# A hybrid decoder layer's HGRN2 head in blocks of 128 tokens, its steps one granule sooner, and the down stage ended bank by bank

## The chip, the cores and the metric

One Trainium2 chip; the program runs on one core of it. The metric is the device time of an execution in microseconds. The profile is that of one execution, which has a time of its own.

## The reference

One inference step of one decoder layer, for a prompt of 256 tokens and for 8 samples of 8 tokens each with a cache of 2048 positions: T = 320 tokens in all, D_MODEL = 2048. What is computed, cut to what matters:

```python
h = rms_norm(x, norm_mix_pre); u = h @ w_in          # columns: hq hf hi hgate dq dk dv g_hg g_da
# HGRN2, per head (8 heads, dk = dv = 128), chunks of c = 64 tokens
f = lb + (1 - lb) * sigmoid(hf); kin = 1 - f; G = cumsum(log f) within a chunk
qg = q * exp(G); kg = kin * exp(-G)
A = where(causal, qg @ kg.T, 0); o = A @ v + qg @ S_prev
dS = (kin * exp(G_last - G)).T @ v; S = exp(G_last) * S_prev + dS       # chunk after chunk
# differential attention: softmax(map 0) - lam * softmax(map 1), times v; over the cache for the samples
y = (sigmoid(g_hg) * (o_hg @ w_branch_hg) + sigmoid(g_da) * (o_da @ w_branch_da)) @ w_out
x = x + rms_norm(y, norm_mix_post)
gate, up = split(rms_norm(x, norm_ffn_pre) @ w_ffn_up)                   # D_FF = 5632
x = x + rms_norm((silu(gate) * up) @ w_ffn_down, norm_ffn_post)          # y_prompt, y_sample
# also out: new keys and values, and the recurrent states (hgrn_prompt, hgrn_sample)
```

## The kernel before, in words

Everything is held transposed: channels on the 128 partitions, the 320 tokens along the free dimension (256 of the prompt, then 64 of the samples). Weights stream in as granules of 128 x 1024 numbers. ACT copies a granule into w_hi (rounded to a shorter float), DVE forms w_lo = raw - w_hi, and TensorE adds the three products hi*hi, lo*hi and hi*lo: 24 matmuls of 320 columns for each granule. There are 4 pairs of buffers (HALVES), so ACT may split granule r once TensorE has used granule r - 4; the semaphores are hi_ready, lo_ready and granule_used. Each engine has its order of work written out by hand, in Python loops that are unrolled and in Fori loops on the chip.

After seven sets of eight granules come eight rounds, one for each head and sample (act_round, vec_round, pe_round, lines 853 to 975). A full round has granules A0 to A7 (a merge-gate set), then D0 to D7 (the next head's set); the last round has no D. Between granules TensorE does the small work of head r (pe_head(q) stands behind granule Aq) and the attention of sample r over its 16 cache pages: scores(g) behind A1, A3, A5 and D0, turn() with 16 transposes of the probabilities behind D2, values(g) behind D3 to D6. On ACT and DVE, act_head(q) and vec_head(q) stand behind the split of granule Aq; vec_head(9) behind D1's split and vec_head(10) behind D2's. vec_pages "most" (lines 759 to 764) forms the row maximum once the last scores are copied, ACT's L708 is the exponential, and turn() waits for it.

The small work of a head, in the names of the code: "i_t" and "kd_t" turn values and decayed keys to have tokens on partitions, five transposes of 64 tokens each; "a" are five products kg x qg; copy_predicated puts them under a causal mask into aT; "ds" are four products that give each chunk's state sum; state[1..4] follow on DVE; "pv" is the attention of the prompt; "ds_s0" and "ds_s1" (lines 624 and 628) give the state sums of samples 0 to 3 and 4 to 7; "o" (lines 632 to 638) sums masked products, states and, for the samples, s0. new_state (line 540) forms the samples' new states, four DVE operations for each half.

At the end, the down stage goes over 44 granules twice (down, line 1213), with eight banks for eight output tiles in each pass. act_out copies the banks into ffn, act_out_sq squares them, vec_squares sums, a product with ones sums over partitions (line 1440), root and reciprocal follow, and four parts of four tiles are scaled, added to the residual and stored (lines 1397 to 1404, 1275).

## Time and profile before

| what | us |
|---|---|
| median of 3 runs | 2168.47 (2166.37 to 2170.33) |
| profiled execution | 2171.54 |
| its span, first to last instruction | 2170.0 |
| TensorE busy (PE) | 2089.6 (96%) |
| weight loads (PEld) | 1954.7 (90%) |
| VectorE busy (DVE) | 1048.1 (48%) |
| ScalarE busy (ACT) | 809.2 (37%) |
| GpSimd busy (POOL) | 74.1 (3%) |

A busy share is the time in which at least one instruction of the engine ran, over the span. Matmuls are pipelined: one of 320 columns is shown 309 ns long but the next begins 147 ns after it, so busy time says that the engine had work, not how fast it went; the distance from start to start does. The granted clock (PEclk) is TensorE's, as a share of 2.4 GHz. PE is the matmuls, PEld the weight loads. Rows of the timeline merge instructions of one line that follow each other on one engine. The seven full rounds lie between 216 and 865 us, the last to 943; branches and output projection follow to 1190, the up projection from there, and the down stage ends at 2140.

### The profile page before, as it was taken

The page shows a single profiled execution, that of the slowest core. Times are in us where ns is not written, and L with a number is a line of the kernel's source. Part 1 is how long each engine was busy: PE and PEld are TensorE (multiplying, and loading weights), DVE is VectorE, ACT ScalarE, POOL GpSimd, SP SyncE. Part 2 cuts the span into 40 slices and gives each one's busy share as a digit, 9 for nine tenths or more (in the row PEclk, how much of TensorE's full clock was granted, in tenths as well). Part 3 has the DMA queues.
Part 4 walks back from the last instruction along what each step waited for, and adds up shares of the span by engine and source line. Part 5 has one row for each costly group of instructions (what it writes and reads, how often), then busy time and mean ns, then how long its engine had stood idle before and what let it go on. Part 6 is the DMA issues. An engine that isn't in the chain of part 4 may idle for free.

```text
span 2170.0 us, 38477 instructions
## 1 busy us (share of the span) xinstructions
PE 2089.6 (96%) x14722; PEld 1954.7 (90%) x14722; DVE 1048.1 (48%) x1323; ACT 809.2 (37%) x1051; POOL 74.1 (3%) x118
## 2 busy tenths in 40 slices
PE   7999999999999999969998899999999999999994
PEld 6999878888888888759998899999999999999994
DVE  6433544536455354555544644444444445445445
ACT  5323343424335242344333433233333333445432
POOL 1001010010100101000000000000000000000000
PEclk9999999999999999989999999999999999999997
DMA  7777686968769687765643244444444444444431
GB/s 251 163 235 240 253 326 246 358 253 338 292 255 354 257 338 298 270 249 193 230 150 124 91 155 146 153 155 155 145 150 149 146 154 144 147 154 145 150 121 48
DMA packets 123842, 443.85 MB, mean 205 GB/s; under 512 B 14485, under 2 KB 18597, under 8 KB 123728
## 3 DMA queue, kind: packets, MB, share of 16 engines
q1 hardware_dynamic: 113872, 403.78, 52.2%
q0 software_dynamic: 9920, 39.38, 6.1%
q8 instruction: 33, 0.54, 0.1%
q14 instruction: 17, 0.14, 0.0%
HBM read 423.19 MB, written 22.54 MB: 205 GB/s over the span
## 4 chain that ended last, share of the span: by engine, by line
PE 92%; DVE 3%; DMA 2%; ACT 1%; issue 1%; DVEq 0%; SPq 0%; ACTq 0%
PE ps L388 23%; PE ps L390 22%; PE ps L389 22%; PE ps L1432 5%; PE ps L1431 5%; PE ps L1433 5%; PE ps L809 3%; DMA raw<-w_in 2%; PE ps L843 2%; PE ps L638 1%; PE ps L818 1%; DVE n_rs L776 0%; PE ps L632 0%; DVE w_lo L347 0%; PE ps L634 0%
## 5 line engine op out<-in xcount | busy, mean ns | idle before, releaser
L347 DVE TENSOR_TENSOR w_lo<-raw,w_hi 128x1024 fp32r<-128x1024 f32 x416 | 504.5, 1223 | 587.3 <-ACT w_hi L342 293.6
L388 PE MATMUL ps<-x_hi,w_hi 128*128 128x320 f32 x1408 | 454.3, 323 | 17.7 <-DVE w_lo L347 10.6
L388 PE MATMUL ps<-h_hi,w_hi 128*128 128x320 f32 x1408 | 436.0, 310 | 11.2 <-DVE h_lo L1371 10.6
L389 PE MATMUL ps<-x_hi,w_lo 128*128 128x320 f32 x1408 | 442.0, 314 | 0.0
L390 PE MATMUL ps<-x_lo,w_hi 128*128 128x320 f32 x1408 | 441.5, 314 | 0.0
L389 PE MATMUL ps<-h_hi,w_lo 128*128 128x320 f32 x1408 | 435.1, 309 | 0.0
L390 PE MATMUL ps<-h_lo,w_hi 128*128 128x320 f32 x1408 | 435.0, 309 | 0.0
L342 ACT ACTIVATE w_hi<-raw 128x1024 fp32r<-128x1024 f32 x240 | 250.3, 1056 | 417.6 <-PE ps L390 417.6
L388 PEld LDWEIGHTS ps<-x_hi,w_hi 128*128 128x128 f32 x1408 | 271.4, 193 | 64.3 <-issue 49.2
L388 PEld LDWEIGHTS ps<-h_hi,w_hi 128*128 128x128 f32 x1408 | 264.6, 188 | 13.2 <-ACT stage L1307 11.5
L389 PEld LDWEIGHTS ps<-x_hi,w_lo 128*128 128x128 f32 x1408 | 271.6, 193 | 0.0
L390 PEld LDWEIGHTS ps<-x_lo,w_hi 128*128 128x128 f32 x1408 | 270.9, 192 | 0.0
L389 PEld LDWEIGHTS ps<-h_hi,w_lo 128*128 128x128 f32 x1408 | 264.7, 188 | 0.2
L390 PEld LDWEIGHTS ps<-h_lo,w_hi 128*128 128x128 f32 x1408 | 264.6, 188 | 0.0
L1431 PE MATMUL ps<-hid_hi,w_hi 128*128 128x320 f32 x704 | 217.3, 309 | 0.0
L1432 PE MATMUL ps<-hid_hi,w_lo 128*128 128x320 f32 x704 | 217.2, 309 | 0.0
L1433 PE MATMUL ps<-hid_lo,w_hi 128*128 128x320 f32 x704 | 217.2, 309 | 0.0
L370 ACT ACTIVATE w_hi<-raw 128x1024 fp32r<-128x1024 f32 x120 | 126.1, 1051 | 114.6 <-DMA raw<-w_in 98.1
L1431 PEld LDWEIGHTS ps<-hid_hi,w_hi 128*128 128x128 f32 x704 | 132.0, 187 | 0.1
L1433 PEld LDWEIGHTS ps<-hid_lo,w_hi 128*128 128x128 f32 x704 | 132.0, 187 | 0.0
L1432 PEld LDWEIGHTS ps<-hid_hi,w_lo 128*128 128x128 f32 x704 | 132.0, 187 | 0.0
L1383 DVE TENSOR_TENSOR hid_lo<-hidden,hid_hi 128x320 fp32r<-128x320 f32 x88 | 43.3, 492 | 154.8 <-ACT w_hi L1322 154.4
(261 smaller groups left out, 2314.2 us busy)
## 6 DMA issues: line engine op xcount, KB each, us to landing
raw<-w_in SPq DMA_DIRECT2D x176, 512.0 KB, 7.4
raw<-w_up SPq DMA_DIRECT2D x176, 512.0 KB, 3.3
raw<-ck SPq DMA_DIRECT2D x128, 512.0 KB, 6.1
raw<-cv SPq DMA_DIRECT2D x128, 512.0 KB, 7.1
raw<-w_dn SPq DMA_DIRECT2D x88, 512.0 KB, 3.3
raw<-w_out SPq DMA_DIRECT2D x32, 512.0 KB, 4.2
uT<-stage POOLq DMA_DIRECT2D x14, 640.0 KB, 3.7
raw<-w_hg SPq DMA_DIRECT2D x16, 512.0 KB, 4.4
```

The lines of the kernel that those rows point to most:

```text
L342: act.activation(w_hi[slot % HALVES][:, :], raw[slot][:, :], ACT.Copy).then_inc(hi_ready, 1)
L347: dve.tensor_tensor(w_lo[half][:, :], raw[slot][:, :], w_hi[half][:, :].bitcast(F32), ALU.subtract).then_inc(lo_ready, 1)
L370: act.activation(w_hi[q % HALVES][:, :], raw[ring_of(r).slot[kind, q]][:, :], ACT.Copy).then_inc(hi_ready, 1)
L388: pe.matmul(out, wh[:, c, m, :], xh(c), start=first, stop=False)
L389: pe.matmul(out, wl[:, c, m, :], xh(c), start=False, stop=False)
L390: mm = pe.matmul(out, wh[:, c, m, :], xl(c), start=False, stop=last)
L809: ins = pe.matmul(ps[32 * j:32 * j + 32, 7, :], q_rows[:, h, :], raw_all[:, at:at + QUAD, h * PAGE:(h + 1) * PAGE], start=e == 0, stop=e == 1)
L843: ins = pe.matmul(ps[32 * j:32 * j + 32, 6, 0:2 * DV], p_keys[:, p, 32 * j:32 * j + 32], raw[slot][:, 2 * DV * j:2 * DV * (j + 1)], start= ...
L1383: dve.tensor_tensor(hid_lo[slot % HALVES][:, :], hidden[:, bass.ds(k, 1), :].rearrange("p a t -> p (a t)"), hid_hi[slot % HALVES][:, :].bi ...
L1431: pe.matmul(ps[:, m, 0:T], wh[:, c], xh, **dict(add, start=q == 0))
L1432: pe.matmul(ps[:, m, 0:T], wl[:, c], xh, **add)
L1433: ins = pe.matmul(ps[:, m, 0:T], wh[:, c], xl, **dict(add, stop=q >= 3))
```

## The change

In the head, the tokens are taken in blocks of 128, 128 and 64 instead of five of 64: i_tok, kd_tok, aT and the mask are [128, ...]. i_t and kd_t are three transposes each, "a" three products under a mask that is zero outside the two chunks on the diagonal. The state sums of two chunks of one block are products over rows 0 to 63 and rows 64 to 127, into banks 4 and 6. The two sums of the samples are products over rows 0 to 31 and 32 to 63, into banks 6 and 5, with one own_part instead of two. The bank of "a" and of pd's transposes is 5, pv's is 6. Each step stands one granule sooner where it can: kd_t and a behind A3, ds and pd_t behind A4, pv behind A5, the chunks' o behind A6, the samples' part and ds_s behind A7. vec_head(9) only copies o; vec_head(10) forms all eight new states.

In the down stage, the last three granules of the second pass are taken together, bank after bank, with nine products for each bank and granule triple; the last turn of the loop is written out for it. ACT squares each bank from PSUM as it is done, DVE adds each square. The sum product is two of 160 columns in banks 0 and 1. ffn's first eight tiles have been scaled by their gains between the passes (act_out_gain), so the first two output parts need one operation of 1280 columns; the other eight are scaled straight from PSUM. The last part of four tiles is two of two.

```diff
@@ act_head
             if q == 4:
                 act.wait_ge(h_pe.sem, h_pe.at(h, "i_t"))
-                act.activation(i_tok[:, 0:4, :], ps[0:CHUNK, 6, :].rearrange("p (c d) -> p c d", c=4), ACT.Copy)
-                h_act.done(act.activation(i_tok[:, 4, :], ps[0:CHUNK, 4, 3 * P:4 * P], ACT.Copy), "i_tok")
+                h_act.done(by_token(act, i_tok, 6), "i_tok")
+            if q == 5:
+                act.wait_ge(h_pe.sem, h_pe.at(h, "kd_t"))
+                h_act.done(by_token(act, kd_tok, 4), "kd_tok")
             if q == 6:
...
+                act.wait_ge(h_pe.sem, h_pe.at(h, "pd_t"))
...
+        def by_token(act, dst, bank):
+
+            act.activation(dst[:, 0:2, :], ps[:, bank, 0:2 * P].rearrange("p (c d) -> p c d", c=2), ACT.Copy)
+            return act.activation(dst[0:CHUNK, 2, :], ps[0:CHUNK, bank, 2 * P:3 * P], ACT.Copy)
@@ vec_head
-            if q == 4:
+            if q == 3:
                 dve.wait_ge(h_act.sem, h_act.at(h, "eG"))
...
             if q == 9:
                 dve.wait_ge(h_pe.sem, h_pe.at(h, "o"))
-                new_state(0, 6)
                 h_vec.done(dve.tensor_copy(o_hg[:, bass.ds(h, 1), :].rearrange("p a t -> p (a t)"),
                                            ps[:, 4, 0:T]), "o")
             if q == 10:
-                dve.wait_ge(h_pe.sem, h_pe.at(h, "ds_s1"))
-                new_state(1, 5)
+                dve.wait_ge(h_pe.sem, h_pe.at(h, "ds_s"))
+                new_state(0, 6)
+                h_vec.done(new_state(1, 5), "s_new")
@@ pe_head
-            if q == 4:
+            if q == 3:
                 pe.wait_ge(h_vec.sem, h_vec.at(h, "qkd"))
...
+                h_pe.done(to_tokens(kd, 4), "kd_t")
+                for t0, n in NT:
+                    ins = pe.matmul(ps[0:n, 5, t0:t0 + n], kg[:, t0:t0 + n], qg[:, t0:t0 + n], start=True, stop=True)
+                h_pe.done(ins, "a")
+            if q == 4:
                 pe.wait_ge(h_act.sem, h_act.at(h, "kd_tok"))
                 for c in seq:
-                    ins = pe.matmul(ps[:, 4, c * DV:(c + 1) * DV], kd_tok[:, c, :], i_tok[:, c, :],
-                                    start=True, stop=True)
+                    at = c // 2 * DV
+                    ins = pe.matmul(ps[:, 4 + 2 * (c % 2), at:at + DV], kd_tok[rows[c], c // 2, :],
+                                    i_tok[rows[c], c // 2, :], start=True, stop=True)
                 h_pe.done(ins, "ds")
...
+                for j, (t0, n) in enumerate(NT):
+                    pe.matmul(ps[:, 4, t0:t0 + n], i_tok[0:n, j, :], aT[0:n, t0:t0 + n], start=True, stop=True)
+                    for c in ((1,), (2, 3), ())[j]:
+                        pe.matmul(ps[:, 4, span[c]], state[:, c - 1, :], qg[:, span[c]], start=False, stop=True,
+                                  skip_group_check=True)
             if q == 7:
...
                 h_pe.done(ins, "o")
+                pe.wait_ge(h_act.sem, h_act.at(h, "o_att"))
+                for b in range(2):
+                    t = slice(32 * b, 32 * b + 32)
+                    ins = pe.matmul(ps[:, 6 - b, :], kd_tok[t, 2, :], i_own[t, :, :], start=True, stop=True)
+                h_pe.done(ins, "ds_s")
@@ down
+                turns = (DOWN - 4) // 8 - pas
+                with eng.Fori(0, turns) as i:
                     for q in range(4, 12):
-                        one(8 * i + q, q, i)
+                        one(8 * i + q, q, i, do)
+                if pas:
+                    for q in range(4, 12):
+                        one(8 * turns + q, q, turns, end if end and q > 11 - MERGED else do)
...
+        def act_out_gain(act):
+            act.wait_ge(g_act.sem, g_act.at(0, "q1"))
+            for m in range(8):
+                ins = act.activation(ffn[:, m, :], ffn[:, m, :], ACT.Copy, scale=nrm_w[:, 3, m:m + 1])
+            g_act.done(ins, "w")
...
+        def act_end_sq(act):
+
+            act.wait_ge(g_vec.sem, g_vec.at(0, "s1"))
+            for m in range(8):
+                if m < 7:
+                    act.wait_ge(down_done, 7 * 5 + 7 * 4 + m + 1)
+                else:
+                    act.wait_ge(granule_used, R_DOWN + 2 * DOWN)
+                t_act.done(act.activation(stage[m // 4][:, m % 4, :], ps[:, m, 0:T], ACT.Square), f"q{m}")
+
+        def vec_end_sq(dve):
+            for m in range(8):
+                dve.wait_ge(t_act.sem, t_act.at(0, f"q{m}"))
+                t_vec.done(dve.tensor_tensor(sq_sum[:, :], sq_sum[:, :], stage[m // 4][:, m % 4, :], ALU.add), f"s{m}")
...
@@ act_rest
                 if pas and q == 1:
-                    act_out(act, 0)
+                    act_out(act)
+                if pas and q == 2:
+                    act_out_sq(act)
                 if pas and q == 3:
-                    act_out_sq(act, 0)
+                    act_out_gain(act)
@@ pe_rest
+            def down_end(pas, k, r, slot, use, q):
+
+                if q < 11:
+                    return
+                pe.wait_ge(lo_ready, r + 1)
+                for m in range(8):
+                    c = slice(P * m, P * m + P)
+                    for back in range(MERGED - 1, -1, -1):
+                        at = (slot - back) % HALVES
...
```

How instructions stand on the engines. The first place is VectorE in a full round, from the split of D1 to the end of the maximum (L760 is "near", L764 the negated maximum; L347, L349 are splits). Before:

```order
L347 TENSOR_TENSOR w_lo<-raw,w_hi 128x1024 [waits hi_ready]
L540 SCALAR_TENSOR_TENSOR s<-s,eG,ps 128x128 [waits h_pe]
L540 SCALAR_TENSOR_TENSOR s<-s,eG,ps 128x128 x3
L565 COPY o_all<-ps 128x320
L347 TENSOR_TENSOR w_lo<-raw,w_hi 128x1024 [waits hi_ready]
L540 SCALAR_TENSOR_TENSOR s<-s,eG,ps 128x128 [waits h_pe]
L540 SCALAR_TENSOR_TENSOR s<-s,eG,ps 128x128 x3
L760 TENSOR_TENSOR s_all<-ps,near 128x128 [waits k_act]
L762 TENSOR_REDUCE mxk<-s_all 128x1 [waits k_vec]
```

And of the change, the same stretch:

```order
L349 TENSOR_TENSOR w_lo<-raw,w_hi 128x1024 [waits hi_ready]
L564 COPY o_all<-ps 128x320
L349 TENSOR_TENSOR w_lo<-raw,w_hi 128x1024 [waits hi_ready]
L540 SCALAR_TENSOR_TENSOR s<-s,eG,ps 128x128 [waits h_pe]
L540 SCALAR_TENSOR_TENSOR s<-s,eG,ps 128x128 x7
L759 TENSOR_TENSOR s_all<-ps,near 128x128 [waits k_act]
L761 TENSOR_REDUCE mxk<-s_all 128x1 [waits k_vec]
```

The four states that stood behind D1's split now stand behind D2's, ahead of the maximum.

The second place is TensorE behind granule A7 of a round: the end of the head's part. Before (its last sample sum, L628, stands behind D0 and the scores L809):

```order
L632 MATMUL ps<-aT,i_tok 128x64 [waits h_vec]
L632 MATMUL ps<-aT,i_tok 128x64
L634 MATMUL ps<-qg,state 128x64
...
L635 MATMUL ps<-aT,i_tok 128x64
L638 MATMUL ps<-qg,s 128x8 x8
...
L809 MATMUL ps<-raw,q_rows 32x512 [waits k_act]
L809 MATMUL ps<-raw,q_rows 32x512 x7
...
L628 MATMUL ps<-i_own,kd_tok 128x512 [waits h_vec]
```

Of the change, from behind A6 to behind A7:

```order
L625 MATMUL ps<-aT,i_tok 128x128
L627 MATMUL ps<-qg,state 128x64
L625 MATMUL ps<-aT,i_tok 128x128
L627 MATMUL ps<-qg,state 128x64 x2
L625 MATMUL ps<-aT,i_tok 128x64
...
L632 MATMUL ps<-qg,s 128x8 x8
...
L638 MATMUL ps<-i_own,kd_tok 128x512 [waits h_act]
L638 MATMUL ps<-i_own,kd_tok 128x512
```

The chunks' part has moved one granule up, and both sample sums stand behind the eight-column products (L632 in the change).

The third place is ScalarE at the end of the program (L1237, L1245 before, L1266 after; L1332 and L1354 are the root). Before:

```order
L1237 ACTIVATE ffn<-ps 128x320 [waits down_done] x7
L1237 ACTIVATE ffn<-ps 128x320 [waits granule_used]
L1245 ACTIVATE stage<-ffn 128x1280 [waits g_vec,g_act]
L1245 ACTIVATE stage<-ffn 128x1280
L1332 ACT_TABLE_LOAD
L1332 ACTIVATE rs_mix<-ps,eps_c 128x320 [waits y_pe]
```

Of the change:

```order
L1266 ACTIVATE stage<-ps 128x320 [waits down_done,g_vec]
L1266 ACTIVATE stage<-ps 128x320 [waits down_done] x6
L1266 ACTIVATE stage<-ps 128x320 [waits granule_used]
L1354 ACT_TABLE_LOAD
L1354 ACTIVATE rs_mix<-ps,eps_c 128x320 [waits y_pe]
```

Copies and squares have become one step for each bank.

## Rows read from the trace of the kernel before

**Rows 1.** Windows: stretch, its us, busy time (instructions) by engine, PEclk, DMA share, GB/s.
```profile
654.53:747.32 92.79, 92.74 (x709) 77.08 (x707) 45.58 (x81) 36.51 (x59) 6.31 (x10) 0.96 0.79 297
747.32:838.72 91.40, 91.16 (x709) 75.47 (x707) 45.58 (x81) 36.57 (x59) 6.34 (x10) 0.98 0.80 304
728.75:735.58 6.83, 6.83 (x30) 6.83 (x30) 1.52 (x5) 0.00 (x0) 0.00 (x0) 0.50 0.20 73
824.32:827.74 3.42, 3.42 (x15) 3.42 (x14) 0.66 (x2) 0.00 (x0) 0.00 (x0) 0.50 0.00 0
925.70:930.10 4.40, 3.68 (x16) 3.27 (x16) 0.65 (x1) 1.30 (x3) 0.00 (x0) 0.50 0.72 259
930.13:933.50 3.37, 2.97 (x53) 1.80 (x57) 0.77 (x3) 1.89 (x3) 0.00 (x0) 1.00 0.31 86
```

**Rows 2.** Timeline, TensorE, rounds 4 and 5: start us, us, engine, line, shapes, count.
```profile
637.28 1.95 PE L638 MATMUL ps<-qg,s 128*128 128x8 f32 x16
...
713.11 1.16 PE L611 MATMUL ps<-i_tok,kd_tok 64*128 64x128 f32 x8
...
725.68 0.66 PE L632 MATMUL ps<-aT,i_tok 64*128 64x64 f32 x4
726.27 0.43 PE L634 MATMUL ps<-qg,state 128*128 128x64 f32 x2
...
728.45 3.34 PE L638 MATMUL ps<-qg,s 128*128 128x8 f32 x16
...
738.97 1.12 PE L628 MATMUL ps<-i_own,kd_tok 64*128 64x512 f32 x2
...
747.16 1.91 PE L818 MATMUL ps<-ident,s_all 128*128 128x128 f32 x16
```

**Rows 3.** Timeline, TensorE, the two maps' scores of the prompt, round 5.
```profile
687.73 0.50 PE L590 MATMUL ps<-mk,mq 64*128 64x128 f32 x4
688.06 0.61 PE L591 MATMUL ps<-mk,mq 64*128 64x256 f32 x4
```

**Rows 4.** Timeline, VectorE and ScalarE ahead of turn(), round 5.
```profile
741.81 1.12 DVE L540 SCALAR_TENSOR_TENSOR s<-s,eG,ps 128x128 f32<-128x128 f32 x4
...
742.84 0.28 DVE L760 TENSOR_TENSOR s_all<-ps,near 128x128 f32<-128x128 f32 x1
...
744.27 2.02 ACT L708 ACTIVATE s_all<-s_all,mxk 128x2056 f32<-128x2056 f32 x1 [3.64 <-DVE mxk L764]
...
747.35 1.23 DVE L347 TENSOR_TENSOR w_lo<-raw,w_hi 128x1024 fp32r<-128x1024 f32 x1 [3.12 <-ACT w_hi L370]
```

**Rows 5.** Timeline, between the two down passes; the last is granule q = 4's first product.
```profile
1988.54 2.43 ACT L1245 ACTIVATE stage<-ffn 128x1280 f32<-128x1280 f32 x2
...
1990.45 2.50 DVE L1104 TENSOR_REDUCE sq_part<-stage 128x320 f32<-128x1280 f32 x1
...
1997.26 1.22 DVE L1385 TENSOR_TENSOR w_lo<-raw,w_hi 128x1024 fp32r<-128x1024 f32 x1
...
1999.47 0.31 PE L1431 MATMUL ps<-hid_hi,w_hi 128*128 128x320 f32 x1
```

**Rows 6.** Timeline, the end of the program.
```profile
2137.39 3.52 ACT L1237 ACTIVATE ffn<-ps 128x320 f32<-128x320 f32 x8 [9.48 <-PE ps L1433]
...
2143.39 1.28 ACT L1332 ACT_TABLE_LOAD   x1
...
2147.50 0.49 DVE L1106 TENSOR_TENSOR sq_sum<-sq_sum,sq_part 128x320 f32<-128x320 f32 x1
2148.05 1.44 PE L1440 MATMUL ps<-sq_sum,ones 128*128 128x320 f32 x2 [7.62 <-DVE sq_sum L1106]
...
2150.15 2.15 DVE L1397 RECIPROCAL rs_mix<-rs_mix 128x320 f32<-128x320 f32 x1 [2.16 <-ACT rs_mix L1332]
2152.34 1.94 DVE L1400 SCALAR_TENSOR_TENSOR ffn<-ffn,nrm_w,rs_mix 128x320 f32<-128x320 f32 x4
...
2164.81 1.49 DVE L1404 TENSOR_TENSOR ffn<-o_all,ffn 128x1280 f32<-128x1280 f32 x1
```

More of the change, by code:

```diff
@@ L282, in build @@
         HEAD_LOADS = 16 * 6
-        h_pe = Steps(sem("h_pe"), "scores vk i_t kd_t a ds pd_t pv ds_s0 o ds_s1", 1)
+        h_pe = Steps(sem("h_pe"), "scores vk i_t kd_t a ds pd_t pv o ds_s", 1)
         h_act = Steps(sem("h_act"), "ef tok lg eG p i_tok kd_tok pdt o_att", 1)
-        h_vec = Steps(sem("h_vec"), "fg kin s max nmax G Gd qkd rc rcl pd2 pd own0 aT st1 st2 st3 st4 own1 s_new0 o s_new1", 1)
+        h_vec = Steps(sem("h_vec"), "fg kin s max nmax G Gd qkd rc rcl pd2 pd own aT st1 st2 st3 st4 o s_new", 1)
         passed = sem("passed")
@@ L574, in pe_head, with to_tokens @@
             span = [slice(CHUNK * c, CHUNK * (c + 1)) for c in range(CHUNKS)]
-            def five(src, bank, rest, col):
+            rows = [slice(CHUNK * (c % 2), CHUNK * (c % 2) + CHUNK) for c in seq]
+            def to_tokens(src, bank):
                 pe.sem_inc(passed, 1)
-                for c in range(CHUNKS):
-                    out = ps[0:CHUNK, bank, c * P:(c + 1) * P] if c < 4 else ps[0:CHUNK, rest, col:col + P]
-                    ins = pe.transpose(out, src[:, span[c]], ident[:, :])
+                for j, (t0, n) in enumerate(NT):
+                    ins = pe.transpose(ps[0:n, bank, j * P:(j + 1) * P], src[:, t0:t0 + n], ident[:, :])
                 return ins
@@ L598, in pe_head @@
                 pe.wait_ge(h_act.sem, h_act.at(h, "tok"))
-                pe.wait_ge(h_vec.sem, h_vec.at(h, "s"))
-                h_pe.done(five(x[:, 2, :], 6, 4, 3 * P), "i_t")
-            if q == 4:
-                pe.wait_ge(h_vec.sem, h_vec.at(h, "qkd"))
-                pe.wait_ge(h_act.sem, h_act.at(h, "i_tok"))
-                h_pe.done(five(kd, 4, 5, T), "kd_t")
-                for c in range(CHUNKS):
-                    ins = pe.matmul(ps[0:CHUNK, 5, span[c]], kg[:, span[c]], qg[:, span[c]], start=True, stop=True)
-                h_pe.done(ins, "a")
@@ L1436, in down_granule @@
                 ins.then_inc(granule_used, 1)
-            down(pe, down_granule)
-            pe.wait_ge(g_vec.sem, g_vec.at(1, "s1"))
-            y_pe.done(pe.matmul(ps[:, 0, 0:T], ones[:, :], sq_sum[:, :], start=True, stop=True), "ss")
+            def down_end(pas, k, r, slot, use, q):
[6 more added lines that the diff above has]
+                        at = (slot - back) % HALVES
+                        xh, xl = hid_hi[at][:, :], hid_lo[at][:, :]
+                        add = dict(start=False, stop=True, skip_group_check=True)
+                        pe.matmul(ps[:, m, 0:T], w_hi[at][:, c], xh, **add)
+                        pe.matmul(ps[:, m, 0:T], w_lo[at][:, c], xh, **add)
+                        ins = pe.matmul(ps[:, m, 0:T], w_hi[at][:, c], xl, **add)
+                        if m == 7:
+                            ins.then_inc(granule_used, 1)
+                    if m < 7:
+                        ins.then_inc(down_done, 1)
+            down(pe, down_granule, down_end)
+            pe.wait_ge(t_vec.sem, t_vec.at(0, "s7"))
+            for e in range(2):
+                own = slice(T // 2 * e, T // 2 * e + T // 2)
+                ins = pe.matmul(ps[:, e, T:T + T // 2], ones[:, :], sq_sum[:, own], start=True, stop=True)
+            y_pe.done(ins, "ss")
         def pool_rest(pool):
@@ L1690 @@
     same = (i[:, None] // NQ == i[None, :] // NQ).astype(np.int32)
+    causal = np.zeros((P, T), np.int32)
+    for c in range(SEQ // CHUNK):
+        t0 = c % 2 * CHUNK
+        causal[t0:t0 + CHUNK, CHUNK * c:CHUNK * c + CHUNK] = tri
+    causal[0:CHUNK, SEQ:T] = tri * same
     hot = np.zeros((33, BIAS_L), np.float32)
```

162 lines of the change are left out of this document (73 added, 89 removed).

## The prediction

> **What bounds the kernel now.** I read the stretches by window first. They show the profiled execution's 93 us rounds: TensorE is busy in all of both rounds shown (92.74 of 92.79 us, 91.16 of 91.40), VectorE in half, and the difference between the two rounds is clock: 0.96 against 0.98 granted [rows 1]. Then the timeline of one round, r = 5. So what TensorE is given to do, at which clock, and the few places where it has no slack decide a round. Seven rounds are full ones; the eighth has no granules D. At the end of the program nothing overlaps any more: from the last product on, the last copies, squares, sums, root, reciprocal and four output parts follow each other [rows 6].
>
> Two facts of these rows carry the argument. First the clock. In round 5 TensorE runs at 0.50 (1.2 of 2.4 GHz) from 728.75 to 735.58, in round 6 from 824.32 to 827.74 [rows 1]. Each fall comes while TensorE is in, or just behind, its sparsest stretch, the state block after granule A7: small products L632 to L635 and then L638 with eight columns each. The 16 instructions of L638 take 1.95 us at full clock and 3.34 us when it fell [rows 2]. Half clock costs half its duration, so 3.4 us in round 5 and 1.7 in round 6. The two rounds differ by 1.39 us, near the 1.7 of the difference. By their lengths and clock the seven full rounds have five long falls and two short ones: 5 x 3.4 + 2 x 1.7 = 20.5 us, 2.9 a round. Second, a chain at turn(): scores s3 end at 738.97 (the start of L628), ACT copies them and splits D2's weights, DVE splits D2, forms four states (L540), corrects and reduces the row maximum (from L760), ACT takes the exponential L708, and only then may TensorE transpose (L818) [rows 2, 4].
>
> **The change part by part, in a full round.**
>
> Products. L611 has 8 instructions in 1.16 us at K = 64, so about 0.11 us each beyond the first latency [rows 2].
> - i_t, kd_t and a: ten transposes become six, five products three. Eight instructions fewer, some of them 64 columns wide: estimate -0.4 us.
> - ds keeps its four products, but neighbours now stand in rows 0 to 63 and 64 to 127, with different banks. The scores do that already: L590 and L591, eight instructions of 128 and 256 columns, span from 687.73 to 688.67, 0.94 us [rows 3], where at the 0.11 us per 128 columns of L611 they would need 0.4 + 0.9 + latency 0.2 = 1.5. Pairs run beside each other. I take -0.45; the bounds are 0 and -0.55 (half of 1.1).
> - o: the pieces before L638 go from 725.68 to 728.45, 2.77 us, for 16 instructions. Two of one kind cost about 0.16 + 0.20, because each change between K = 64 and K = 128 shows up: L632 at 725.68 (four) needs 0.59, L634 0.36 [rows 2]. After: 12 instructions, one such change instead of seven, 12 x 0.11 + 0.25 = 1.56. That is -1.2.
> - Sample states: L624 and L628 are two instructions each, 1.05 us before the next may start (L628 shows 1.12 with its tail) [rows 2], 2.1 together. After, two products of K = 32 in rows 0 to 31 and 32 to 63, banks 6 and 5. Taken as a pair: 1.1 us, -1.0. Bounds 0 and -1.05. For K = 32 no row exists, the nearest is the K = 64 pair of [rows 3].
>
> The Trainium skill, "TensorE: Matmul & The Clock Gate", Part 3, lets small products in different row groups run concurrently, K = 32 included; by it the last line would be exactly one product's time, 1.05. The trace agrees for K = 64 and has nothing for K = 32.
>
> Sum of the products: -0.4 - 0.45 - 1.2 - 1.0 = -3.05 us a round.
>
> The turn. L628 stood behind s3 and took 1.05 us of TensorE there; it is now ahead of D0. TensorE then reaches turn() 747.16 - 738.97 - 1.05 = 7.14 us after s3. The chain does not get shorter, it gets longer: new_state(0) has left its idle place in D1 and stands between D2's split and L760, so eight L540 instead of four. Four take 742.84 - 741.81 = 1.03 us [rows 4]. Queued behind them on DVE are the maximum, for which ACT waits, and D3's split. L708 ended at 744.27 + 2.02 = 746.29, 7.3 us after s3, with the readout of its sum 7.4; now 8.4. TensorE waits 1.3 us. Its transposes (1.7 us to the next start, 1.91 with the tail [rows 2]) end at 10.1; D3's split L347 ended at 747.35 + 1.23 = 748.58 [rows 4], 9.6 after s3, now 10.65. TensorE waits 0.55 more. Together +1.9 us. This is the stall that replaces the work taken away. Bounds: 0 (if the order on DVE turned out harmless) and 2.6. Per round -3.05 + 1.9 = -1.15; seven rounds -8.0.
>
> Steps one granule sooner. The products qkd, the copies kd_tok and pdt and the states each move with the TensorE step that they serve, so every hand-over keeps its distance of one granule or more. I cost it at 0; the cover is that DVE is busy 45.58 us and ACT 36.51 of the round's 92.79 [rows 1]. If it were gone, the first wait would be TensorE's for aT, which now stands ahead of pd's transposes: at most one split, 1.2 us a round. The page loads follow the scores, whose spacing after s3 does not shrink; what stands from D3 to the next A0 is untouched, so the just-in-time weight loads there keep their distance.
>
> Clock. The state block is cut in two: 1.56 us after A6 and L638 with its pair, 1.75 + 1.1 = 2.85 us at full clock after A7, with a dense granule between, instead of 4.5 in one piece. The falls should be fewer and shorter, not gone, because L638 itself is unchanged and its columns are the fewest. From 2.9 us a round I take 1.7. The new idle 1.3 and 0.55 us at the turn may cost a fall now and then: 0.4. Net -0.8 a round, -5.6. Bounds: -20 (no falls) and +24 (below).
>
> The last round has no granules to hide in: TensorE waits for L708. The products save 3.05 less the 1.05 of L628, which there lay beside nothing that counts but behind s3; from s3 to L760 the way shrinks from L628 and four L540 (2.2 us) to ACT's copy, about 0.75. 1.95 - 0.1 + 1.45 = 3.3; I take -3.0.
>
> Between the passes of the down stage. ACT now squares ahead of granule q = 3 and scales eight tiles behind it. Before, ACT split q = 3 ahead of the squares: w_hi was done as L1245 began, 1988.6, and DVE had its half done as L1104 began, 1990.45. Now the 2.43 us of L1245 stand ahead of that split: w_hi at 1988.6 + 2.4 = 1991.0, DVE's half (1.22 for w_lo, 1.6 with hid_lo) at 1992.6. DVE's two reductions are queued behind it and start 2.1 us late, and behind them is the split for q = 4, which ended at 1997.26 + 1.22 = 1998.48, now 2000.6. TensorE wants q = 4 at 1999.47 [rows 5]. Wait plus restart: +1.35 us, once. The eight scaled copies (L1237: eight in 3.52 [rows 6]) end before that on ACT and hide. Merging the last three granules makes TensorE wait for the split of the very last one when only one granule of products lies between that split's start and the wait, not three. A granule is 24 products, 3.52 us at their spacing of 0.147; the split is w_hi and w_lo with their halves of hidden, about 1.5 + 1.7 us and two handovers. So nearly even: +0.2, with bounds 0 and 2.
>
> The end. Before: last copy ends at 2137.39 + 3.52 = 2140.91, then squares, reductions, sum product, root, and the first L1400 at 2152.34 [rows 6], 11.4 us later. After: at 2140.91 the last square ends (a square in place of the copy); one add 0.49; the sum product, four instructions of 160 columns at a clock that has had no time to fall, 0.7 (1.44 at half clock before); by then ACT's table load 1.28 is just done; root with its handovers 2150.15 - 2149.49 = 0.66; reciprocal 2.15; 0.1 for the two handovers left: 0.49 + 0.7 + 0.66 + 2.15 + 0.1 = 4.1. That is -7.3. Output parts: before 2152.34 to 2166.30, 13.96. After: four operations of 128x1280 at 1.49 (parts 0 and 1), 1.94 + 1.49, and twice 0.97 + 0.8, with gaps 13.2: -0.75. The last store is 320 KB instead of 640 and 3.7 us stood between the last add and the span's end: -0.45. Sum -8.5, bounds -9.5 and -6.5.
>
> **Sum.** -8.0 - 5.6 - 3.0 + 1.35 + 0.2 - 8.5 = -23.55. The profiled execution took 2171.54 us (span 2170.0), so 2148.0; the median of the runs is 3.07 lower, so **2144.9**.
>
> **Rivals.**
> - The clock holds through the state block: 2.9 instead of 0.8 a round comes back, 14.7 more: 2130. For it: the long piece is broken. Against: L638 alone is 1.75 us with eight columns.
> - The row tiles do not pair and the clock does what it did: 7 x 1.45 + 5.6 = 15.8 less gain: 2161. For it: no K = 32 row. Against: [rows 3].
> - The clock falls at the turn, shortly, in every round: 1.7 - 0.4 = 1.3 a round, 9 us: 2154. For it: two idle pieces round a block of transposes. Against: the clock rose from 0.50 to 1.00 at 930.13 when TensorE had, from 925.70, done 16 transposes and waited 1.1 us [rows 1], so transposes hold it up. In the Trainium skill, "TensorE: Matmul & The Clock Gate", Part 4, a transpose does not count as busy the way a product does; by that rule this rival would be the forecast. The trace disagrees.
> - Slower: the same fall, but of the long kind, 6.8 us as in five of seven rounds now, 3.4 us of loss, and nothing comes back at the state block: -23.55 + 7 x 3.4 + 5.6 = +5.9: 2174. It decides from 3.4 us a round upward. For it: 3.6 us from the start of the wait to D3 in which TensorE does only transposes. Against: the same row at 930.13.
> - The change does not do what it says at the end, the root waiting for something else: +7, 2152; only the table load is near, and it is 1.28 long.
>
> **Chances.** Forecast 0.48 (its own range 2137 to 2153), clock holds 0.15, no pairs 0.15, short fall at the turn 0.12, end not shortened 0.03, slower 0.05, something near nothing 0.02. A difference under 0.2%, 4.3 us, is what a measurement of this kernel can't tell from none. Faster 0.92, same 0.03, slower 0.05. Range: from the clock case to the one without pairs, 2131 to 2162.
>
> **What would show it.** TensorE idle before L818 of about 1.3 us and before D3's first product of 0.5, in each full round; eight L540 in a row right ahead of the maximum; rounds of 90 to 91 us; the K = 32 products starting within 0.05 us of each other; clock falls behind the eight-column products, in some rounds; one wait of 1.3 us some 14 us into the second down pass; the first output product about 4 us after the last square. Wrong if the rounds stay at 92 us or more, or if the falls move to the turn.

## The result, and the profile after

The changed kernel takes 2129.7 us, median of four executions (2127.3 to 2134.0), beside 2167.4 us for the kernel before on the same chip. The ratio is 0.983, 95% interval 0.9815 to 0.9846: 1.7% faster. The forecast was 2144.9 us with a range from 2131 to 2162; the sign was right, the time is 15 us below the forecast and just under the range.

The profiled execution of after took 2133.98 us (span 2132.4, 37.6 less than before's). It is the slowest of the four and has the lowest mean granted clock, 0.981 against 0.984 and 0.985; e12 below takes the same kernel again.

A fall is a stretch in which TensorE's granted clock is 0.50; a short one lasts 3.4 us, a long one 6.8.

Windows of after, one row a round from turn to turn (the 16 transposes of L817, which was L818), last a stretch at half clock. Columns as in [rows 1].

```profile
279.36:368.69 89.33, 86.58 (x695) 72.11 (x695) 45.15 (x81) 35.95 (x59) 6.36 (x10) 1.00 0.84 315
368.69:458.06 89.37, 87.93 (x695) 73.43 (x695) 45.14 (x81) 35.95 (x59) 6.35 (x10) 0.98 0.82 311
458.06:545.91 87.85, 86.41 (x695) 72.11 (x695) 45.09 (x81) 35.94 (x59) 6.32 (x10) 1.00 0.83 315
545.91:635.21 89.30, 87.87 (x695) 73.64 (x695) 45.09 (x81) 35.95 (x59) 6.34 (x10) 0.98 0.84 310
635.21:723.00 87.79, 86.35 (x694) 72.11 (x695) 45.09 (x81) 36.07 (x59) 6.33 (x10) 1.00 0.84 314
723.00:812.26 89.26, 87.83 (x695) 73.65 (x695) 45.10 (x81) 35.95 (x59) 6.35 (x10) 0.98 0.83 310
812.26:893.66 81.40, 76.98 (x622) 61.71 (x623) 41.72 (x78) 33.06 (x56) 6.32 (x10) 0.97 0.86 324
797.15:800.56 3.41, 3.41 (x14) 3.41 (x14) 0.00 (x0) 0.00 (x0) 0.00 (x0) 0.50 0.33 120
```

Rounds of 87.8 us without a fall of the clock alternate with rounds of 89.3 with a short one. Before, every round had a fall, mostly of 6.8 us [rows 1]. TensorE is no longer busy all the time: 1.44 us of each round are idle, 1.26 ahead of the transposes and 0.17 behind them. The first row, 89.33 at clock 1.00, holds 1.3 us more of idle time, mostly a wait for a weight split (DVE's w_lo, 1.08 us at 306.61).

Timeline of after, TensorE, the state block of round 5, which answers to [rows 2]:

```profile
700.90 0.38 PE L625 MATMUL ps<-aT,i_tok 128*128 128x128 f32 x2
701.12 0.33 PE L627 MATMUL ps<-qg,state 128*128 128x64 f32 x2
701.29 0.44 PE L625 MATMUL ps<-aT,i_tok 128*128 128x128 f32 x2
701.57 0.56 PE L627 MATMUL ps<-qg,state 128*128 128x64 f32 x4
702.05 0.43 PE L625 MATMUL ps<-aT,i_tok 64*128 64x64 f32 x2
...
706.03 1.85 PE L632 MATMUL ps<-qg,s 128*128 128x8 f32 x16
707.80 1.13 PE L638 MATMUL ps<-i_own,kd_tok 32*128 32x512 f32 x4
```

The products of o stand 1.5 us behind A6, the eight-column products (now L632) behind A7. The four instructions of the two K = 32 products take together what the two of one K = 64 product took before, 1.13 us against 1.12.

The turn, answering to [rows 4]: VectorE's D2 split and what is queued behind it, ScalarE's exponential, TensorE's transposes.

```profile
716.13 1.23 DVE L349 TENSOR_TENSOR w_lo<-raw,w_hi 128x1024 fp32r<-128x1024 f32 x1 [7.29 <-ACT w_hi L372]
717.27 2.15 DVE L540 SCALAR_TENSOR_TENSOR s<-s,eG,ps 128x128 f32<-128x128 f32 x8
...
720.77 2.01 ACT L707 ACTIVATE s_all<-s_all,mxk 128x2056 f32<-128x2056 f32 x1 [4.67 <-DVE mxk L763]
...
723.00 1.96 PE L817 MATMUL ps<-ident,s_all 128*128 128x128 f32 x16 [1.26 <-ACT s_all L707]
```

Between the down passes (first product of granule q = 4, now waiting, as [rows 5]) and at the end ([rows 6]):

```profile
1970.48 0.41 PE L1457 MATMUL ps<-hid_hi,w_hi 128*128 128x320 f32 x1 [1.04 <-DVE w_lo L1407]
...
2111.24 0.30 PE L1477 MATMUL ps<-hid_lo,w_hi 128*128 128x320 f32 x1
2111.58 0.44 ACT L1266 ACTIVATE stage<-ps 128x320 f32<-128x320 f32 x1 [0.88 <-PE ps L1477]
2112.04 1.28 ACT L1354 ACT_TABLE_LOAD   x1
2112.12 0.49 DVE L1271 TENSOR_TENSOR sq_sum<-sq_sum,stage 128x320 f32<-128x320 f32 x1 [0.82 <-ACT stage L1266]
2112.67 0.81 PE L1487 MATMUL ps<-sq_sum,ones 128*128 128x160 f32 x4 [1.12 <-DVE sq_sum L1271]
2114.15 2.15 DVE L1419 RECIPROCAL rs_mix<-rs_mix 128x320 f32<-128x320 f32 x1 [1.53 <-ACT rs_mix L1354]
2116.33 1.49 DVE L1423 TENSOR_TENSOR ffn<-ffn,rs_mix 128x1280 f32<-128x1280 f32 x1
...
2128.88 0.82 DVE L1430 TENSOR_TENSOR ffn<-o_all,ffn 128x640 f32<-128x640 f32 x1
```

From the last square (ends 2112.02) to the first output operation are 4.3 us, where it had been 11.4 from the last copy.

**Where the 37.6 us come from.** The start of the last turn moved from 925.74 to 893.66, -32.1; from there to the down stage 1.9 are given back; pass boundary +1.3; from the last copy or square to the span's end 29.1 became 20.4, -8.7. A fall costs less than half its length: 1.5 us for a short one (89.30 - 87.8 here, 92.71 - 91.30 before), so 2.9 for a long one (1.5 + 1.4). In the seven full rounds before: 5 x 2.9 + 2 x 1.5 = 17.5 us; after, four short ones, 6.0. So 11.5 are clock, 7 x 2.0 = 14.0 are products less stall, the last round to its turn gives 5.8 (1.4 of it because its fall was long before and is short after), and 0.8 is left over, below what loads that come late in single rounds move.

The 1.9 us behind the last turn are mostly clock, and not in the transposes. The first 64 products of the values, before; then the stretch at half clock and the same products, after:

```profile
930.73 3.66 PE L843 MATMUL ps<-raw,p_keys 128*32 128x256 f32 x64
```

```profile
892.72:902.96 10.24, 8.19 (x57) 5.33 (x61) 1.45 (x3) 4.13 (x7) 0.00 (x0) 0.50 0.70 260
898.75 5.71 PE L842 MATMUL ps<-raw,p_keys 128*32 128x256 f32 x64
```

In both kernels TensorE waits over 4 us, does the 16 transposes at half clock (4.8 us to the next start) and waits 1.11. Before, the clock was back at 1.00 from 930.13 [rows 1], ahead of the values' products; after, it stayed at 0.50 until 902.96.

### The profile page after: what moved, and what is told of

It reads as the page before. It is cut to its first block, busy times and chain, and to the rows that moved or that the text cites. A ratio compares the mean times of both kernels' runs of the same rounds, so it can differ in the third digit from the quotient of the medians.

```text
span 2132.4 us, 38205 instructions
## 1 busy us (share of the span) xinstructions
PE 2050.7 (96%) x14628; PEld 1926.2 (90%) x14628; DVE 1041.9 (49%) x1322; ACT 805.8 (38%) x1057; POOL 74.2 (3%) x118
## 4 chain that ended last, share of the span: by engine, by line
PE 90%; DVE 5%; ACT 2%; issue 2%; DMA 1%; ACTq 0%; DVEq 0%; SPq 0%
PE ps L390 23%; PE ps L391 22%; PE ps L392 22%; PE ps L1457 4%; PE ps L1458 4%; PE ps L1459 4%; PE ps L808 3%; PE ps L842 3%; DVE w_lo L349 1%; ACT w_hi L372 1%; DVE s L540 1%; PE ps L632 1%; DMA raw<-w_in 1%; PE ps L638 0%; DVE mixed L1386 0%
## 5 line engine op out<-in xcount | busy, mean ns | idle before, releaser
L349 DVE TENSOR_TENSOR w_lo<-raw,w_hi 128x1024 fp32r<-128x1024 f32 x416 | 504.6, 1223 | 620.3 <-ACT w_hi L344 294.0
L390 PEld LDWEIGHTS ps<-h_hi,w_hi 128*128 128x128 f32 x1408 | 264.7, 188 | 13.4 <-ACT stage L1328 11.5
L1457 PE MATMUL ps<-hid_hi,w_hi 128*128 128x320 f32 x680 | 210.0, 309 | 1.0 <-DVE w_lo L1407 1.0
L1458 PE MATMUL ps<-hid_hi,w_lo 128*128 128x320 f32 x680 | 209.8, 309 | 0.0
L1459 PE MATMUL ps<-hid_lo,w_hi 128*128 128x320 f32 x680 | 209.8, 309 | 0.0
L1457 PEld LDWEIGHTS ps<-hid_hi,w_hi 128*128 128x128 f32 x680 | 127.5, 187 | 1.4 <-DVE w_lo L1407 1.3
L1458 PEld LDWEIGHTS ps<-hid_hi,w_lo 128*128 128x128 f32 x680 | 127.5, 187 | 0.0
L1459 PEld LDWEIGHTS ps<-hid_lo,w_hi 128*128 128x128 f32 x680 | 127.5, 187 | 0.0
```

What stands on the lines that cost most here:

```text
L349: dve.tensor_tensor(w_lo[half][:, :], raw[slot][:, :], w_hi[half][:, :].bitcast(F32), ALU.subtract).then_inc(lo_ready, 1)
L390: pe.matmul(out, wh[:, c, m, :], xh(c), start=first, stop=False)
L1457: pe.matmul(ps[:, m, 0:T], wh[:, c], xh, **dict(add, start=q == 0))
L1458: pe.matmul(ps[:, m, 0:T], wl[:, c], xh, **add)
L1459: ins = pe.matmul(ps[:, m, 0:T], wh[:, c], xl, **dict(add, stop=q >= 3))
```

## The experiments

Median, ratio to before with its interval, and the clock falls of the seven full rounds in the profiled execution. Before: 2 short and 5 long; after: 4 short (0.983).

| Run | Median us | Ratio (95%) | Falls |
|---|---|---|---|
| e1 down stage alone | 2160.9 | 0.9967 (0.9955-0.9979) | 3 short, 4 long |
| e2 head alone | 2136.1 | 0.9854 (0.9836-0.9872) | 3 short |
| e3 states early | 2113.0 | 0.9743 (0.9729-0.9756) | 2 short |
| e4 one piece | 2139.8 | 0.9870 (0.9854-0.9885) | 4 short, 2 long |
| e5 half the samples sooner | 2125.7 | 0.9810 (0.9797-0.9822) | none |
| e6 no pair | 2148.6 | 0.9905 (0.9882-0.9928) | 5 long |
| e7 o in eight products | 2146.3 | 0.9899 (0.9882-0.9916) | 2 short |
| e8 pass boundary | 2132.6 | 0.9841 (0.9828-0.9854) | 3 short |
| e9 e3 and e8 | 2112.4 | 0.9744 (0.9731-0.9757) | 2 short |
| e10 e3, e5 and e8 | 2107.2 | 0.9726 (0.9713-0.9739) | none |
| e11 e10, end of one granule | 2108.9 | 0.9730 (0.9717-0.9744) | none |
| e12 after again | 2130.9 | 0.9834 (0.9820-0.9847) | 3 short |

Executions of one program differ in how many rounds have a fall, so a median mixes them and the profile shows one. The runs come from three chips (e1 to e4, e5 to e8, e9 to e12); the kernel before took 2166.2 to 2167.8 us in the median beside them.

**e1 and e2, the change in two halves.** e1 takes only the edits of the down stage, e2 only the rest.

> The kernel before with the down stage of the change alone (squares off the banks, merged last three granules, output parts, gains at the pass boundary); the head is the old one. If the terms read from the trace of after add up: from the last copy or square to the end 20.4 us instead of 29.1 (-8.7), and one wait of about 1.0 us between the passes, so -7.7 us against before, ratio 0.9965. Rounds of 91.3 to 94 us and clock falls as before: five long and two short in the full rounds. Rival: part of the end's gain hangs on something else of the change; then less than -5.

> The change's head with the old down stage. If the parts add up: -37.6 + 7.7 = -30 us against before, ratio 0.986, full rounds of 87.8 us without a fall and 89.3 with a short one, no wait of TensorE between the passes. Rival: the number of clock falls differs from one build to another by chance; then rounds of 87.8 us with a long fall (91.2) turn up as well and the gain is 20 to 26.

By the ratios -7.2 and -31.6 us, together 38.8 against after's 37: the parts add within their intervals. In e1 the last add (2137.48) to the first output operation (2141.69) is after's distance; nothing of the end's gain hangs on the head. In e2 no long fall turned up.

**e3, the sample states one granule sooner.**

```diff
                 if q == 1:
                     vec_head(dve, 9, r)
+                    vec_head(dve, 10, r)
                 if q == 2:
-                    vec_head(dve, 10, r)
                     vec_pages(dve, r, "most")
```

> After, with the eight L540 and their s_new moved one granule forward, behind D1's split and the copy of o, where new_state(0) stood before. Theory: TensorE's wait of 1.26 us ahead of its 16 transposes and the 0.47 us that the transposes take longer both go, -1.7 us in each of seven full rounds, -12 us against after, ratio to before about 0.977; in the last round, where the row maximum is on the path, -2 more. Rival: DVE is then late with D2's split (3.1 us of work ahead of it instead of 1.0) and TensorE waits 0.5 to 1 us before D2: -0.7 a round, -5. Rival on the clock: without the short idle at the turn nothing changes in the falls (they come behind the eight-column products).

Windows of e3, two rounds; then D2's split, the exponential and the transposes.

```profile
534.82:622.11 87.29, 87.29 (x697) 73.62 (x695) 45.60 (x81) 36.07 (x59) 6.31 (x10) 0.98 0.85 317
622.11:707.87 85.76, 85.76 (x697) 72.09 (x694) 45.61 (x81) 36.07 (x59) 6.34 (x10) 1.00 0.86 323
```

```profile
702.42 1.23 DVE L349 TENSOR_TENSOR w_lo<-raw,w_hi 128x1024 fp32r<-128x1024 f32 x1 [4.99 <-ACT w_hi L372]
...
704.99 2.01 ACT L707 ACTIVATE s_all<-s_all,mxk 128x2056 f32<-128x2056 f32 x1 [2.60 <-DVE mxk L763]
...
707.87 1.91 PE L817 MATMUL ps<-ident,s_all 128*128 128x128 f32 x16
```

The round without a fall goes from 87.8 to 85.77, TensorE busy in all of it, and the transposes wait for nothing. VectorE had been idle 4.99 us before D2's split, so the rival's late split did not come. Sixteen to eighteen us against after, more than the 12 expected: 2.0 instead of 1.7 a round, 2.2 in the last round (79.24), and two falls fewer. That the falls became fewer speaks against the last sentence of the expectation, but after itself shows three or four of them, so this is not shown to come from the idle time. One row more: the fall in the round of 87.29 cost 1.52 us.

**e4, the state block in one piece.** Both calls of the round stay; only the step of o's products changes.

```diff
-            if q == 6:
+            if q == 7:
                 for j, (t0, n) in enumerate(NT):
                     pe.matmul(ps[:, 4, t0:t0 + n], i_tok[0:n, j, :], aT[0:n, t0:t0 + n], start=True, stop=True)
```

> After, with the products of o (i_tok x aT and state x qg) moved from behind A6 to behind A7, so that they stand right ahead of the eight-column products: the same instructions, the state block in one piece again. Theory (the cut of the block, with a dense granule between, is what keeps the clock up): falls come back to 2 to 3 us of loss a round, five or more of seven long ones, +9 to +14 us against after, ratio 0.987 to 0.990. Rival (the falls became fewer because the block holds less sparse work in total): within 2 us of after, ratio 0.983 to 0.984, falls short and in every other round.

Timeline of e4, TensorE, a block in which a long fall begins; windows of the round with it, of one with a short fall, and of the long fall.

```profile
436.88 0.43 PE L625 MATMUL ps<-aT,i_tok 64*128 64x64 f32 x2
437.24 1.95 PE L632 MATMUL ps<-qg,s 128*128 128x8 f32 x16
439.12 1.92 PE L638 MATMUL ps<-i_own,kd_tok 32*128 32x512 f32 x4
```

```profile
366.53:457.44 90.91, 89.47 (x695) 74.49 (x695) 45.24 (x81) 36.05 (x59) 6.35 (x10) 0.96 0.81 304
457.44:546.73 89.29, 87.86 (x694) 73.65 (x695) 45.23 (x81) 36.05 (x59) 6.32 (x10) 0.98 0.82 310
439.30:446.10 6.80, 6.80 (x23) 5.30 (x23) 0.49 (x1) 0.00 (x0) 0.00 (x0) 0.50 0.17 65
```

The same instructions cost 10.1 us more (8.9 against e12's median), as the theory had it, though with fewer long falls than it asked for. Falls came back to six of seven full rounds, two of them long: 4 x 1.5 + 2 x 2.9 = 11.8 us, against 6.0 in after and 4.5 in e12. So by the profiled executions the cut is worth some 6 to 7 us of clock. All four executions of e4 have mean clocks of 0.977 and 0.978, the nine of after and e12 0.981 to 0.985; what the medians hold beyond the 6 to 7 us is not placed. The cut is not everything: in one piece, the block with fewer small products still loses 11.8 where before lost 17.5.

**e5, four of the eight sample products one granule sooner.**

```diff
-            if q == 7:
-                for b in range(NB):
+            if q in (6, 7):
+                for b in range(4) if q == 6 else range(4, NB):
...
+            if q == 7:
                 h_pe.done(ins, "o")
```

> After, with four of the eight eight-column products of L638 (x8 of x16) issued one granule sooner, behind the products of o; the other four stay behind A7. Same instructions; the sparsest piece is 0.9 + 1.06 us instead of 1.78 + 1.06. Theory (a fall comes behind the eight-column products if enough of them stand together): no short falls in the full rounds, -1.7 us in each of the four that had one, -6.8 us against after, ratio to before 0.980. Rival (it is the total of sparse work in both places, or the piece behind A6 with its 1.5 + 0.9 us becomes the sparse one): falls in as many rounds or more, 0 to +7 us, ratio 0.983 to 0.986.

Not one fall in the full rounds; the mean clocks of its five executions are 0.985 to 0.987. Windows of e5, two rounds:

```profile
454.12:541.98 87.86, 86.43 (x694) 72.12 (x695) 45.10 (x81) 36.04 (x59) 6.31 (x10) 1.00 0.84 313
629.96:718.51 88.55, 86.58 (x695) 72.11 (x695) 45.10 (x81) 35.88 (x59) 6.31 (x10) 1.00 0.84 312
```

Against after -4.1 us, against e12 -5.2, where three or four short falls are 4.5 to 6.0. In the second row 0.6 us are idle time on late loads, which takes back a part.

**e6 and e7, more work in the two pieces.** e6 takes both sample-state products from the same rows; e7 forms o in eight products, K = 64 and K = 128 in turn, instead of six (the expectation counts one too many).

```diff
-                    t = slice(32 * b, 32 * b + 32)
+                    t = slice(0, 32)
```

```diff
-                for j, (t0, n) in enumerate(NT):
-                    pe.matmul(ps[:, 4, t0:t0 + n], i_tok[0:n, j, :], aT[0:n, t0:t0 + n], start=True, stop=True)
...
+                for c in seq:
+                    pe.matmul(ps[:, 4, span[c]], i_tok[0:CHUNK, c // 2, :], aT[0:CHUNK, span[c]], start=True,
+                              stop=c == 0)
+                    if c:
+                        pe.matmul(ps[:, 4, span[c]], state[:, c - 1, :], qg[:, span[c]], start=False, stop=True)
+                pe.matmul(ps[:, 4, span[4]], i_tok[0:CHUNK, 2, :], aT[0:CHUNK, span[4]], start=True, stop=True)
```

> After, with both products of the sample states taken from rows 0 to 31, so that they cannot run beside each other (the states of the last four samples then come from the wrong rows). Theory (two K = 32 products in rows 0 to 31 and 32 to 63 run at the same time, 1.06 us for both): the block becomes 2.1 us, +1.05 a round, eight rounds +8.4 us by duration; the clock: more busy time of the same products behind the eight-column ones, falls as in after or one or two more, 0 to +4. Ratio 0.987 to 0.989. Rival (the pair ran one after the other and was short for K = 32): no change, 0.983.

> After, with o formed again in nine products, K = 64 and K = 128 in turn, behind A6 (all products of 64 rows taken from rows 0 to 63, so the odd blocks of 64 tokens get wrong values); the block stays cut in two. By the rows of before (2.77 us for these 16 instructions plus 8 changes, against 1.51 now): +1.26 a round, +10 in eight rounds. Theory on the clock (where the work stands decides, not how much): falls as in after, so +10, ratio 0.9875. Rival (the amount of sparse work in the two pieces decides): falls in every round or long ones, 3 to 7 us more, ratio 0.989 to 0.991.

Timeline of e6, the pair's place in a round without a fall and in one with; windows of both rounds. Then of e7, the end of the piece behind A6, a fall behind it and the eight-column products (L633) that follow, and two rounds.

```profile
353.37 1.98 PE L638 MATMUL ps<-i_own,kd_tok 32*128 32x512 f32 x4
...
714.57 2.87 PE L638 MATMUL ps<-i_own,kd_tok 32*128 32x512 f32 x4
```

```profile
369.42:458.21 88.79, 87.35 (x694) 72.46 (x695) 45.10 (x81) 35.92 (x59) 6.37 (x10) 1.00 0.84 312
641.68:733.74 92.06, 90.48 (x695) 74.85 (x695) 45.10 (x81) 35.97 (x59) 6.34 (x10) 0.96 0.81 300
```

```profile
705.79 0.43 PE L629 MATMUL ps<-aT,i_tok 64*128 64x64 f32 x2
706.76:710.17 3.41, 3.41 (x15) 3.41 (x14) 0.98 (x2) 0.00 (x0) 0.00 (x0) 0.50 0.94 381
711.32 1.85 PE L633 MATMUL ps<-qg,s 128*128 128x8 f32 x16
```

```profile
458.91:548.06 89.15, 87.71 (x699) 72.92 (x699) 45.10 (x81) 35.96 (x59) 6.33 (x10) 1.00 0.83 312
637.09:728.29 91.20, 89.46 (x698) 74.47 (x699) 45.09 (x81) 36.13 (x59) 6.34 (x10) 0.98 0.82 303
```

The durations are as expected: 1.98 us instead of 1.13 for the pair in the same rows, the round without a fall 88.8 (+1.0); 89.1 for e7 (+1.3). The pair does run side by side. The clock was expected too good in both. e6 has long falls in five of seven rounds; its six executions lie between 2135.1 us at a mean clock of 0.984 and 2153.8 at 0.976. e7's profile has two short falls, but its executions split too: 2136.1 and 2138.9 us at 0.985 and 0.984, four others 2144.9 to 2148.5 at 0.979 to 0.982. The medians lie 18 to 19 us above after's and e12's in e6, 15 to 17 in e7. By duration e6 costs 8 x 1.0 us and e7 8 x 1.3, so some 10 us of e6 and some 5 to 6 of e7 are clock, an estimate that for e7 no trace shows: its profiled execution is one of the two with few falls. Not only where the small products stand but how long each piece lasts counts: for e7 the rival on the clock came true in the median, and for e6 the 0 to +4 us that the theory gave the clock were too few.

Where e7's falls stand tells more. Both come 0.6 us behind o's products of 64 columns and 4.6 us ahead of the eight-column products (706.76 in the rows, and 348.36). Eight columns are not needed for a fall.

**e8, the boundary of the passes.** late(q) is called behind each granule of the second pass's last turn.

```diff
-                if pas and q == 2:
+                if pas and q == 3:
                     act_out_sq(act)
-                if pas and q == 3:
-                    act_out_gain(act)
...
+            def late(q):
+                if q in (4, 5):
+                    act.wait_ge(g_act.sem, g_act.at(0, "q1"))
+                    act_out_gain(act, (4 * q - 16, 4 * q - 12))
```

> After, with ACT's squares of the first pass behind the split of granule q = 3 as before the change, and its eight scaled copies in two halves of four behind the splits of two granules of the last turn of the second pass. Theory: the wait of 1.04 us of TensorE between the passes goes and nothing comes in its place, since a split of 1.4 us and four copies of 1.8 us fit in one granule of 3.52: -1.0 us, ratio lower by 0.0005, to be seen in the trace rather than in the median. Rival: one of the halves delays a split and TensorE waits there, up to +1.

Windows from the up stage's last wait to the last product of the down stage, of after and then of e8:

```profile
1208.77:2111.55 902.78, 901.74 (x6144) 901.13 (x6144) 420.75 (x399) 325.80 (x379) 0.00 (x0) 1.00 0.43 143
```

```profile
1207.89:2109.37 901.48, 901.48 (x6144) 901.13 (x6144) 420.65 (x399) 326.17 (x379) 0.00 (x0) 1.00 0.43 143
```

1.30 us, to be seen nowhere but in this stretch: the median is not below after's (2132.6), as the head's falls and loads vary by more.

**e9 to e11, the edits together.**

> After, with two edits: the eight L540 behind D1's split (2113.0 us by itself) and the squares and scaled copies between the passes laid out so that no split is late. Theory: the two waits have nothing to do with each other, so 1.3 us (the wait of 1.04 and the restart) come off: about 2111.7 us, ratio 0.9737. Rival: the gain at the pass boundary comes back as a wait later in the second pass: 2113.

> The same, and four of the eight eight-column products one granule sooner. Theory (cutting the sparsest piece keeps the clock up in every round, and the terms add): the profiled execution of the first edit alone had two short falls in its full rounds, 3.4 us; without them about 2108.5 us, ratio 0.972; no half clock between the first turn and the last full round. Rival: the state block is not what decides once the turn has no idle time; then as the run before it, 2111 to 2112.

> The same three edits, with only the last granule of the down stage bank by bank (three products a bank instead of nine). Banks then come free every 0.44 us instead of 1.32, and VectorE's add with its hand-over takes about 0.6: the last add would be late by 8 x 0.15 = 1.2 us. Theory: +1.2 us against the three edits (stretch from the last product to the first output operation longer by that), median ratio higher by 0.0005. Rival: the split of the last granule is what the merged form waits for, and one granule alone costs nothing: 0 or -0.2.

Window of e10, one round; then the sum of squares at the end in e10 and in e11.

```profile
274.59:360.37 85.78, 85.78 (x697) 72.11 (x694) 45.14 (x81) 35.96 (x59) 5.75 (x10) 1.00 0.86 324
```

```profile
2084.74 0.81 PE L1493 MATMUL ps<-sq_sum,ones 128*128 128x160 f32 x4 [1.12 <-DVE sq_sum L1274]
```

```profile
2086.95 0.81 PE L1493 MATMUL ps<-sq_sum,ones 128*128 128x160 f32 x4 [1.73 <-DVE sq_sum L1274]
```

e9 cannot be told from e3 in the median; the wait between the passes is gone from its trace, where the down stage takes 310.0 us from its first to its last product instead of 311.3. e10 has six rounds of 85.78 us in a row, no fall in the seven full rounds, and is the fastest kernel of the study: 2107.2 us, 2.7% under before and some 23 us under after. e11 costs 0.6 us more between the last product and the sum, half of what was worked out, and its median is 1.7 us higher with overlapping intervals; merging three granules is a small gain.

**e12, after once more.**

> The changed kernel once more, unchanged: its profiled execution was its slowest (2134.0 us at a mean granted clock of 0.981; the three others 2127.3 to 2129.8 at 0.984 and 0.985). Theory: the rounds are the same and only the number of rounds with a fall differs; an execution near 2129 us has one to three short falls in the full rounds instead of four, and rounds of 87.8 us otherwise. Rival: the difference lies outside TensorE's clock, in waits for loads; then four falls again and a longer wait elsewhere.

Its profiled execution (2129.7 us, clock 0.984) has three short falls; its rounds without one take 88.1 to 88.7, partly idle on late loads. Of the 4.3 us to the first profile 0.9 lie ahead of the first turn and 1.2 from there to the last turn, with one fall fewer (1.5) and a little more waiting. The other 2.3 lie behind the last turn, where the clock was at 0.50 for 10.2 us in the first profile and for 3.4 us in this one. So theory and rival both miss a place: the falls of the last round differ between executions too.

## Why the prediction missed

Each part of the sum had the right sign, and sizes were off, the clock's most; they add up in the profiled executions, where 14.0 us lie between forecast and result. For the clock the reason behind the size was off too. Where a fall of before began, in round 3:

```profile
544.35 3.54 PE L638 MATMUL ps<-qg,s 128*128 128x8 f32 x16
544.43:551.26 6.83, 6.83 (x29) 6.83 (x30) 1.52 (x5) 0.00 (x0) 0.00 (x0) 0.50 0.24 85
```

- **Clock (forecast -5.6, measured -11.5).** The step that failed is "From 2.9 us a round I take 1.7": the falls were taken to stay because the eight-column products were unchanged. They left three of seven rounds and became short in the other four, 0.9 us a round instead of 1.7. The trace of before could have told: the fall at 544.43 came when the eight-column products had hardly begun, behind 2.8 us of o's, and o's products are what the change shortened and moved away. e7's falls say the same. e4 shows that the cut with a dense granule between is worth 6 to 7 us; e6 and e7 show that the clock also hangs on how long each piece lasts, which I counted for its duration alone. These effects are not independent (together they would come to more than 11.5), so no share is shown for each, and why a given round has a fall and the next has none stays open. The price of a fall was also too high: 1.5 and 2.9 us, not 1.7 and 3.4. The rival "the clock holds" comes near in time (2130) but is not what the traces show; it is true of e5 and e10.
- **Products (forecast -3.05, measured -3.4 a round).** From the first start of each group to what follows, round 4 before against round 5 after: o 2.77 to 1.51, the sample states 2.10 to 1.06, ds 1.09 to 0.65, i_t, kd_t and a -0.46, all as forecast within 0.06. Not counted were pd's transposes, 0.48 to 0.31. A further 0.3 stands behind turn_back()'s two transposes, and I cannot place it.
- **The stall (forecast +1.9, measured +1.7).** 1.26 us ahead of the transposes, as forecast with 1.3, and from their start to D3 0.47 more than before (0.17 of it idle), forecast with 0.55. e3 removes it. With products and the 0.3, it is -2.0 a round instead of -1.15: three small misses of one sign, seven times, are 6 us of the error.
- **No fall at the turn.** Right: TensorE's idle 1.26 us and 16 transposes stand in every full round, and each fall of the full rounds came in the state block or behind one of its pieces. The reason given, the row at 930.13, is weak: at the last turn of after the same 16 transposes and the same 1.11 us of waiting left the clock at 0.50 until 902.96. The Trainium skill, "TensorE: Matmul & The Clock Gate", Part 4, says that transposes do not count as busy the way products do; no full round shows an effect of it at this length.
- **Last round (forecast -3.0, measured -3.9).** 5.8 less to its turn, 1.4 of it clock; 1.9 given back behind the turn because the clock stayed low, which e12's profile does not show. So part of this agreement is luck.
- **Pass boundary and merging (forecast +1.55, measured +1.3).** The wait is where it was expected, 1.04 us, and e8 takes it away. The merged products waited for no split.
- **The end (forecast -8.5, measured -8.7).** 4.3 us to the first output operation for 4.1; e1 shows that it stands by itself.

The range's low end was the case in which only the clock did better. That clock and products could both do better was not in it. Two small slips of the sum change nothing: 5 x 3.4 + 2 x 1.7 is 20.4, and 3.05 less 1.05 is 2.0.

## What to carry to other kernels

Where TensorE loses its clock though it is never idle, look at what stands ahead of the start of the fall, not at the smallest products near it: a run of small products may be cut by a dense block, paired in row tiles or brought to fewer changes of K, and here each of these paid a second time through the clock. When TensorE gets less work ahead of a point where it waits for another engine, look at what was moved into the chain that ends there: eight state updates behind the wrong split cost 2 us a round, and one line took them out. Count the falls in more than one execution before pricing them.

## What the hardware showed that was not expected

- The clock fell to 0.50 with TensorE busy all the time, in or just behind runs of small products: with the first product of eight columns (before, 544.43), or behind products of 64 columns alone (e7, 706.76). Whether it does differs between equal rounds of one execution and between executions: one program (e6) took 2135 to 2154 us at mean clocks of 0.984 to 0.976.
- A stretch of 3.4 us at half clock cost 1.5 us, not 1.7: in before's fall at 544.43 the 320-column products of the granule start 0.27 us apart, at full clock 0.147.
- Two K = 32 products of 512 columns in rows 0 to 31 and 32 to 63, to different banks, took 1.13 us together, 1.98 in the same rows.
